# Filling products of a recurrence as four 64x64 quadrants over half the tokens, with three more tiles placed there

## The chip, the cores and the metric

The kernel runs on one core of one Trainium2 chip. The metric is the device time of the whole program in microseconds; the times shown are 3 runs of one and the same program. PE is TensorE, DVE is VectorE, ACT is ScalarE, POOL is GpSimd, SP is SyncE.

## The reference, cut to what matters

Two layers of a decoder trunk over 264 tokens (256 of a prompt and 8 samples). Per layer:

```
h = x @ w_in[l]                       # 2048 -> 10928 columns, all mixers' inputs and gates
rwkv_scan, per head and token:        # mixer A
    sa = S @ a_t
    S  = S * w_t + sa x b_t + v_t x k_t
    y  = S @ r_t
q, kc, vc, ks, vs, kw, vw, gl, z_b = split(fb)      # mixer B: attention, gated per head
merged = sigmoid(g_a) * (o_a @ w_up_a) + sigmoid(g_b) * (o_b @ w_up_b)
y = layer_norm(ALPHA * x + merged @ w_out)
```

Everything is float32. The change touches only how and when columns of `x @ w_in` are computed: those of the gate logits, the queries, z_b, some keys and values, and of g_b.

## The kernel before

A layer holds tokens along the free dimension (T = 264) and model columns on the 128 partitions. A tile is 128 output columns of `x @ w_in`: 16 products of 128x128 weights with 128x264 of XT, summed in one PSUM bank. I call one such product a k-step. A layer runs through these stages on PE:

1. two tiles (`two_tiles`), then 20 pairs of main tiles (`main_pair`);
2. the recurrence of mixer A, in chunks of 64 tokens, for four quads of two head pairs (`for hq in range(NQUAD)`). All its own products are 64x64 quadrants, except two groups at its start (64x128 and 128x128) and two with 32x32 blocks. Their steps are called low, bon, a1, tok, then y1 z1 to y5 z5 (a triangular inverse by doubling; y5 and z5 are the 32x32 ones), then for each of four chunks r, u, s, o;
3. the mixers' stage: the state update of the 8 samples on DVE (`rs`), a group norm, compression, attention of the prompt and of the samples (`as`);
4. gate pairs, up pairs and output pairs (`gate_pair` and so on), and the layer norm.

Steps of stages 2 and 3 depend on each other through ACT and DVE. So that PE isn't idle meanwhile, 44 more tiles of `x @ w_in` are filled in between: after each own step PE calls `project(L, ..., name)`, which goes on with the list TILES up to the k-step that the table UPTO names for that place. UPTO comes from the tables BEHIND (per quad), and BEHIND_MIX (mixers' stage). In the recurrence 20 tiles (EARLY) at most are used up, and the last call there, `project(L, "mixers")`, brings the count up to 20. The last call of the mixers' stage, `project(L, "gates")`, does what is left of the 46 tiles before the first gate pair.

A tile's bank is 6 or 7, by its number's parity, so the next tile can be summed while ACT empties the last one: `take_out` stands in ACT's program at the same named places, waits for `tile_done`, copies to H and raises `tile_out`. `mix` is DVE's counterpart, for the one tile that it mixes. The weights of a tile (1 MB) come through SP into one of two slots of WT, when the tile two before it is done.

Before the first gate pair stand, on the other engines: DVE's copy of the samples' outputs (L2227), two products that make z_b's output (L2230, L2233, the step `zb_v out`), SP's loads of the first pair's four weight blocks, which wait for that step since they overwrite the queries (L497), POOL's two sums of those blocks (L729 and L731, steps s3 and s1), and DVE's two (L2249, L2261, steps s2 and s4). The gate pair is seven products of 8 k-steps over 132 tokens: the first needs block 0, the second block 1, the third s3, the fourth s1, the fifth s2, the last s4.

Of the kernel before, what the change touches and what calls it, by code (L numbers as in the profile page):

```python
# [73 lines left out]
EARLY = 20  # L74
# [43 lines left out]
def plan():  # L118

    upto = {}  # L120
    for L in range(DEPTH):
        first = L * N_TILES * KT
        m = upto[L, "start"] = first + 2 * KT
        m = upto[L, "bc"] = m + 4
        for hq in range(NQUAD):
            for name, n in BEHIND.items():
                m = upto[L, hq, name] = min(m + n + (0 if name != "low" else 9 if hq == 0 else 2 * L), first + EARLY * KT)
        m = upto[L, "mixers"] = first + EARLY * KT
        for name, n in BEHIND_MIX.items():
            m = upto[L, name] = min(m + n, first + N_TILES * KT)  # L130
        upto[L, "gates"] = first + N_TILES * KT
    return upto

# [45 lines left out]
def hybrid_trunk(nc, ins, outs):  # L179
# [4 lines left out]
    with ExitStack() as ctx:  # L184
# [3 lines left out]
        def sem(name):  # L188
            return ctx.enter_context(nc.semaphore(name))
# [167 lines left out]
        scaled = sem("tile_scaled")  # L357
        S = {}
# [120 lines left out]
        def a_tile(L, kind, t):  # L479

            return VF[:, t - V0, :] if kind == "v" and L == 0 else H[:, t, :]

# [275 lines left out]
        def _(pe):  # L758
            mm, tr = nc.tensor.matmul, nc.tensor.transpose
            at = [0]  # L760
# [4 lines left out]
            def project(*place):  # L765

                while at[0] < UPTO[place]:
                    n, k = divmod(at[0], KT)
# [3 lines left out]
                    if k == 0:  # L772
# [3 lines left out]
                    if k == 8:  # L776
                        pe.wait_ge(w_in_slot[s][1], 16 * loads_of_slot(L, i, u))
                    rows, bank, start, stop = slice(0, P), 6 + s, k == 0, k == KT - 1
                    x = XT[:, k, :]
                    if kind == "gl":  # L780

                        rows, start, stop = slice(k % 2 * C, k % 2 * C + C), k < 2, k >= KT - 2
                    ins = mm(PB[rows, bank, 0:T], WT[:, s, k, 0:rows.stop - rows.start], x, start=start, stop=stop)  # L783
                    if k == KT - 1:
                        ins.then_inc(tile_done[s], 1)
                    at[0] += 1

            def two_tiles(L):
# [22 lines left out]
                at[0] += 2 * KT  # L811
# [181 lines left out]
            both = [slice(a * C, a * C + C) for a in range(2)]  # L993
# [11 lines left out]
            for L in range(DEPTH):  # L1005
# [161 lines left out]
                project(L, "mixers")  # L1167
# [265 lines left out]
        def _(sc):  # L1433
# [11 lines left out]
            def take_out(*place):  # L1445

                while (at[0] + 1) * KT <= UPTO[place]:
# [7 lines left out]
                    if kind == "lo":  # L1455
# [3 lines left out]
                    elif kind in ("kv", "q", "zb"):  # L1459
                        act(H[:, t, :], psum, ACT.Copy, scale=SCALE if kind == "q" else 1.0).then_inc(tile_out[s], 1)  # L1460
                    elif kind == "gl":
                        copy(H[:, t, :], psum).then_inc(tile_out[s], 1)
                    else:
                        if kind == "gb" and t == 9:
                            sc.wait_ge(*step("mix_t", L, "v3"))
                            sc.wait_ge(st_kv, 16 * (L + 1))
                        if kind == "ga" and t == 0:
                            sc.wait_ge(*step("gn_v", L, "out"))
                        act(H[:, t if kind == "ga" else GB_AT[t], :], psum, ACT.Tanh, scale=0.5).then_inc(tile_out[s], 1)  # L1469

            for L in range(DEPTH):
# [104 lines left out]
                take_out(L, "mixers")  # L1576
# [176 lines left out]
        def _(ve):  # L1753
            tt, ts, stt = nc.vector.tensor_tensor, nc.vector.tensor_scalar, nc.vector.scalar_tensor_tensor
            cp, red, recip = nc.vector.tensor_copy, nc.vector.tensor_reduce, nc.vector.reciprocal
            at, mixed = [0], [0]
# [4 lines left out]
            def mix(*place):  # L1761

                while (at[0] + 1) * KT <= UPTO[place]:
# [4 lines left out]
                    at[0] += 1  # L1768
                    if kind != "lo":
                        continue  # L1770
# [85 lines left out]
            for L in range(DEPTH):  # L1856
# [23 lines left out]
                for hq in range(NQUAD):  # L1880
# [41 lines left out]
                    v("rk", ins)  # L1922

# [18 lines left out]
                    mix(L, hq, "low")  # L1942
# [19 lines left out]
                    eight = lambda m: spread(small(m).unsqueeze(1), P, 2 * NCH, C)  # L1962
                    wait(("rw_t", "tok"))
# [5 lines left out]
                    for name in ("a1", "tok"):  # L1969
                        mix(L, hq, name)  # L1970
                    for j in range(1, LEVELS + 1):
# [15 lines left out]
                        else:  # L1987
# [4 lines left out]
                            v(f"z{j}", ins)  # L1992
                        mix(L, hq, f"z{j}")
                    if it:
                        ve.wait_ge(st_wkv, it * 32)
                    v("st", nc.vector.memset(ST[:, 0, :, :], 0.0))
# [13 lines left out]
                mix(L, "mixers")  # L2010
# [545 lines left out]
```

## Time and profile before

| | |
|---|---|
| runs | 2153.27, 2157.24, 2158.91 us (median 2157.24) |
| profiled execution | span 2153.9 us from the first to the last instruction; its whole time isn't reported apart |
| PE busy | 2119.7 us, 98% |
| DVE, POOL, ACT busy | 1060.1, 505.5, 412.9 us |
| granted TensorE clock | mean 0.995 |
| recurrence, both layers | about 281 to 510 us and 1346 to 1582 us |

How to read it: every float32 product has two records on PE, each with its weight load; both rows and counts below are of records, so a k-step of a filling tile is 2 records, and a 64x64 quadrant product 2 as well. Busy PE means that some record was under way; a record's duration contains its way through the array, and what a product costs in a row of products is the distance from start to start. For a merged row that is (its duration minus that of one record) divided by (count minus 1).

### The profile page before, as it was taken

How to read it: one execution, taken by the hardware profiler on the slowest of the kernel's cores; microseconds unless marked ns; L12 is line 12 of the kernel's file. 1: busy time of each engine (PE TensorE's matmuls, PEld its weight loads, DVE VectorE, ACT ScalarE, POOL GpSimd, SP SyncE). 2: the span in 40 equal slices, each digit the busy share in tenths (PEclk: the TensorE clock that was granted, in tenths of full speed). 3: DMA queues.
4: the chain of work that ended last, by engine and by line, in shares of the span. 5: the costliest groups of instructions: out<-in, count | busy, mean ns of one | idle time of the engine just before them, and what ended most of it. 6: DMA issues, size and time to landing. Idle time of an engine off the chain costs nothing.

```text
span 2153.9 us, 48812 instructions
## 1 busy us (share of the span) xinstructions
PE 2119.7 (98%) x21488; PEld 1870.9 (87%) x21488; DVE 1060.1 (49%) x1780; ACT 412.9 (19%) x1181; POOL 505.5 (23%) x377
## 2 busy tenths in 40 slices
PE   9999999999999999999999999999999999999997
PEld 8999977777887779999899999777777877899996
DVE  4454344443726524773645543444447165247745
ACT  1111112222103411110211121222221044111002
POOL 3433300002011123333223333000020112134331
PEclk9999999999999999999999999999999999999999
DMA  8545333335543365554355443332365334654551
GB/s 302 170 160 171 119 131 101 101 101 222 195 137 118 110 224 176 165 178 160 126 171 173 157 165 125 115 101 101 101 228 179 119 118 139 218 172 160 173 171 66
DMA packets 88979, 329.50 MB, mean 153 GB/s; under 512 B 11904, under 2 KB 11920, under 8 KB 86464
## 3 DMA queue, kind: packets, MB, share of 16 engines
q1 hardware_dynamic: 74592, 268.60, 37.2%
q0 software_dynamic: 11872, 53.59, 7.1%
q10 hardware_dynamic: 2304, 4.20, 0.6%
q8 instruction: 169, 2.77, 0.5%
q14 instruction: 42, 0.34, 0.1%
HBM read 315.91 MB, written 18.82 MB: 155 GB/s over the span
## 4 chain that ended last, share of the span: by engine, by line
PE 96%; DVE 3%; DMA 1%; issue 0%; ACT 0%; SPq 0%; DVEq 0%
PE PB L783 30%; PE PB L824 3%; PE PB L851 3%; PE PB L847 3%; PE PB L842 3%; PE PB L837 3%; PE PB L827 3%; PE PB L833 3%; PE PB L1239 3%; PE PB L763 1%; PE PB L907 1%; PE PB L989 1%; PE PB L808 1%; PE PB L972 1%; PE PB L974 1%; PE PB L967 1%
## 5 line engine op out<-in xcount | busy, mean ns | idle before, releaser
L783 PE MATMUL PB<-XT,WT 128*128 128x264 f32 (+1 forms) x2816 | 691.5, 395 | 0.1
L783 PEld LDWEIGHTS PB<-XT,WT 128*128 128x128 f32 (+1 forms) x2816 | 509.0, 189 | 101.0 <-issue 15.5
L1438 ACT ACTIVATE VT<-PB 128x132 f32<-128x132 f32 (+2 forms) x280 | 79.1, 291 | 578.3 <-PE PB L837 130.6
L1438 ACT ACTIVATE ARENA<-PB 128x128 f32<-128x128 f32 (+6 forms) x185 | 75.5, 430 | 226.0 <-PE PB L1089 62.2
L618 POOL DMA_DIRECT2D out<-in_c_win x16 | 8.1, 506 | 456.0 <-DVE ARENA L2005 456.0
L618 POOL DMA_DIRECT2D ARENA<-in_c_sel x64 | 40.0, 625 | 234.5 <-issue 234.5
L639 POOL TENSOR_TENSOR TOEP<-WT 128x1024 f32<-128x1024 f32 x20 | 47.3, 2365 | 181.0 <-PE PB L837 139.6
L639 POOL TENSOR_TENSOR TOEP<-H 128x1024 f32<-128x1024 f32 x20 | 48.2, 2408 | 139.5 <-PE PB L837 135.0
L833 PE MATMUL PB<-ARENA,TOEP 128*128 128x132 f32 x640 | 78.5, 276 | 0.0
L837 PE MATMUL PB<-ARENA,TOEP 128*128 128x132 f32 x640 | 78.5, 276 | 0.0
L842 PE MATMUL PB<-ARENA,TOEP 128*128 128x132 f32 x640 | 78.5, 276 | 0.0
L851 PE MATMUL PB<-XT,TOEP 128*128 128x132 f32 x640 | 78.5, 276 | 0.0
L833 PEld LDWEIGHTS PB<-ARENA,TOEP 128*128 128x128 f32 x640 | 75.1, 190 | 0.0
L837 PEld LDWEIGHTS PB<-ARENA,TOEP 128*128 128x128 f32 x640 | 75.1, 190 | 0.0
L842 PEld LDWEIGHTS PB<-ARENA,TOEP 128*128 128x128 f32 x640 | 75.1, 190 | 0.0
L851 PEld LDWEIGHTS PB<-XT,TOEP 128*128 128x128 f32 x640 | 75.1, 190 | 0.0
L1239 PE MATMUL PB<-ARENA 128*128 128x288 f32 x256 | 62.7, 406 | 0.0
L1842 DVE TENSOR_TENSOR VT<-PB,VT 128x264 f32<-128x264 f32 x40 | 17.3, 432 | 91.7 <-PE PB L851 91.7
L1239 PEld LDWEIGHTS PB<-ARENA 128*128 128x128 f32 x256 | 48.6, 190 | 13.3
L1644 ACT ACTIVATE ARENA<-ARENA 128x128 f32<-128x128 f32 (+1 forms) x128 | 56.2, 443 | 17.3 <-DVE ARENA L2164 17.3
L2336 DVE TENSOR_TENSOR VT<-VT 128x132 f32<-128x132 f32 x32 | 47.4, 1520 | 24.1 <-ACT VT L1438 24.1
L1469 ACT ACTIVATE H<-PB 128x264 f32<-128x264 f32 x48 | 18.7, 389 | 209.1 <-PE PB L783 208.9
(456 smaller groups left out, 4165.8 us busy)
## 6 DMA issues: line engine op xcount, KB each, us to landing
WT<-in_w_all SPq DMA_DIRECT2D x340, 512.0 KB, 4.5
H<-in_w_all SPq DMA_DIRECT2D x120, 512.0 KB, 4.5
KNVC<-in_w_all SPq DMA_DIRECT2D x40, 512.0 KB, 3.9
out<-in_c_win POOLq DMA_DIRECT2D x16, 512.0 KB, 4.6
ARENA<-in_c_cmp POOLq DMA_DIRECT2D x64, 128.0 KB, 4.3
ARENA<-in_c_sel POOLq DMA_DIRECT2D x64, 128.0 KB, 4.0
TOEP<-in_toep POOLq DMA_DIRECT2D x2, 2048.0 KB, 9.1
ARENA<-in_states POOLq DMA_DIRECT2D x4, 1024.0 KB, 11.9
```

What stands on the lines that cost most here:

```text
L639: mark("ms_p", it, add(OS1, w[2], w[3], ALU.add), "s1")
L783: ins = mm(PB[rows, bank, 0:T], WT[:, s, k, 0:rows.stop - rows.start], x, start=start, stop=stop)
L824: mm(a, w[0][:, k, :], XT[:, k, t0], start=k == 0, stop=k == BLK - 1)
L827: ins = mm(b, w[1][:, k, :], XT[:, BLK + k, t0], start=False, stop=k == BLK - 1, skip_group_check=True)
L833: mm(c, OS3[:, k, :], MT[:, 2, k, :], start=k == 0, stop=k == BLK - 1)
L837: ins = mm(d, OS1[:, k, :], MT[:, 0, k, :], start=False, stop=k == BLK - 1, skip_group_check=True)
L842: ins = mm(a, OS2[:, k, :], MT[:, 1, k, :], start=False, stop=k == BLK - 1, skip_group_check=True)
L847: ins = mm(c, w[3][:, k, :], MT[:, 3, k, :], start=False, stop=k == BLK - 1, skip_group_check=True)
L851: ins = mm(d, OS4[:, k, :], XT[:, BLK + k, t1], start=False, stop=k == BLK - 1, skip_group_check=True)
L1239: ins = mm(PB[:, 3 * (s // 8) + gp, 0:CMP_N], W1D[:, s, :], x, start=s % 8 == 0, stop=s % 8 == 7)
L1438: return act(out, in_, ACT.Copy)
L1644: ins = act(x, x, ACT.Exp, bias=NM[u % 3][:, t, i:i + 1], accum_out=RSM[u % 3][:, t, i:i + 1])
```

## The change

In tiles 3 to 22 of each layer (FIRST_QUAD to EARLY), `project` replaces a k-step by eight quadrant products: for each half of the tokens (132), each half of the 128 input rows and each half of the 128 output columns. The upper input rows sum into bank 6, the lower into bank 7. Progress is now counted in half k-steps (TILE = 32 of them). A tile now takes two operations out of PSUM: ACT copies bank 6 to H and raises `quad_half`, then DVE adds bank 7 to it and raises `tile_out`. Since a tile uses both banks, PE waits before each of these tiles, and before the one behind them, until the tile before is out. EARLY goes from 20 to 23, the tables of the recurrence are new, and so are the places where DVE's `mix` is called. The recurrence's own products are as before.

```
-EARLY = 20
+EARLY = 23
+FIRST_QUAD = 3
+TILE = 2 * KT
...
-BEHIND = {"low": 16, "bon": 4, "a1": 11, "tok": 7}
-for level in range(1, LEVELS + 1):
-    BEHIND.update({f"y{level}": 1 if level < LEVELS else 2, f"z{level}": 2 if level < LEVELS else 4})
+BEHIND = {"low": 32, "bon": 9, "a1": 23, "tok": 16}
+for level, (y, z) in enumerate(((3, 5), (3, 5), (0, 5), (3, 6), (5, 13)), 1):
+    BEHIND.update({f"y{level}": y, f"z{level}": z})
 for chunk in range(NCH):
-    BEHIND.update({f"r{chunk}": 1, f"u{chunk}": 1, f"s{chunk}": chunk // (NCH - 1)})
+    BEHIND.update({f"r{chunk}": 3 if chunk else 0, f"u{chunk}": 3, f"s{chunk}": chunk // (NCH - 1) * 11})
...
+                        if in_quadrants(n) or n and in_quadrants(n - 1):
+                            pe.wait_ge(tile_out[1 - s], (n - 1) // 2 + 1)
...
+                    if in_quadrants(n):
+                        tokens = slice(h * HALF, h * HALF + HALF)
+                        narrow = kind == "gl"
+                        for ra in both:
+                            for ca in both[k % 2:k % 2 + 1] if narrow else both:
+                                w = WT[ra, s, k, 0:C] if narrow else WT[ra, s, k, ca]
+                                ins = mm(PB[ca, 6 + ra.start // C, tokens], w, XT[ra, k, tokens], start=k <= narrow and h == 0,
+                                         stop=k >= KT - 1 - narrow and h == 1, skip_group_check=True)
...
# take_out, on ACT
+                    if in_quadrants(n):
+                        act(H[:, quad_home(kind, t), :], PB[:, 6, 0:T], ACT.Copy, scale=quad_scale(kind)).then_inc(quad_half, 1)
# mix, on DVE
+                    if in_quadrants(n):
+                        ve.wait_ge(quad_half, joined[0])
+                        stt(home, PB[:, 7, 0:T], quad_scale(kind), home, ALU.mult, ALU.add).then_inc(tile_out[s], 1)
...
# DVE, in a quad: mix(low) moves up, behind the products "rk", in quads 1 to 3
                     v("rk", ins)
+                    if hq:
+                        mix(L, hq, "low")
...
# the remainder of EARLY tiles behind the recurrence is gone
-                project(L, "mixers")
```

By the tables, the filling of quads 1 to 3 goes from 65 k-steps (67 in the second layer) to 160 half k-steps, which is 5 tiles, so that every one of these tiles ends at the end of a named place: low, a1, z2, z5 and s3. In quad 0 tile 2, still whole, ends within the place low.

The first place, on PE: the end of the doubling and the chunks of quad 1 in the first layer (L1144 and L1172 are the steps r, L1150 and L1178 the steps u, L783 and L806 the filling). Before:

```order
L783 MATMUL PB<-XT,WT 128x264 x4
L1144 MATMUL PB<-ARENA 64x64 x4
L783 MATMUL PB<-XT,WT 128x264
L1150 MATMUL PB<-ARENA 64x64 x4
L783 MATMUL PB<-XT,WT 128x264
L1156 MATMUL PB<-ARENA 64x64 x4
L1160 MATMUL PB<-ARENA 64x64 x4
L1163 MATMUL PB<-ARENA 64x64 x4
```

And now:

```order
L806 MATMUL PB<-XT,WT 64x132 x52
L1172 MATMUL PB<-ARENA 64x64 x4
L1178 MATMUL PB<-ARENA 64x64 x4
L806 MATMUL PB<-XT,WT 64x132 x12
L1184 MATMUL PB<-ARENA 64x64 x4
L1188 MATMUL PB<-ARENA 64x64 x4
L1191 MATMUL PB<-ARENA 64x64 x4
```

What moved: 4 whole k-steps before r0 are 13 halves (52 quadrant products), the filling between r0 and u0 is gone, and that behind u0 is three halves in place of a k-step.

The second place, on DVE: the start of quad 1 (L1921 and L1956 are the products "rk", which step bon waits for; L1934 and L1971 the last one that step a1 waits for). Before:

```order
L1921 SCALAR_TENSOR_TENSOR ARENA<-H,PT,ARENA 128x264 x2
L1927 SCALAR_TENSOR_TENSOR ARENA<-KNVC,ARENA 128x4x64 x2
L1931 TENSOR_TENSOR ARENA<-H,ARENA 128x4x64 x2
L1933 TENSOR_TENSOR ARENA<-ARENA 128x512
L1934 TENSOR_TENSOR ARENA<-ARENA 128x512
```

And now:

```order
L1956 SCALAR_TENSOR_TENSOR ARENA<-H,PT,ARENA 128x264 x2
L1803 SCALAR_TENSOR_TENSOR H<-PB,H 128x264
L1964 SCALAR_TENSOR_TENSOR ARENA<-KNVC,ARENA 128x4x64 x2
L1968 TENSOR_TENSOR ARENA<-H,ARENA 128x4x64 x2
L1970 TENSOR_TENSOR ARENA<-ARENA 128x512
L1971 TENSOR_TENSOR ARENA<-ARENA 128x512
```

What moved: the addition that empties bank 7 (L1803) stands among the operations that step a1 waits for.

The third place, on PE: the end of the samples' attention and the first gate pair (L763 there is the transposition whose result DVE copies back, L865 the first product of the pair). Before:

```order
L1382 MATMUL PB<-KNVC,ARENA 32x256 x4
L783 MATMUL PB<-XT,WT 128x264 x3
L763 MATMUL PB<-CM,ARENA 128x128 x2
L783 MATMUL PB<-XT,WT 128x264 x49
L865 MATMUL PB<-XT,H 128x132 x8
L868 MATMUL PB<-XT,H 128x132 x8
```

And now:

```order
L1409 MATMUL PB<-KNVC,ARENA 32x256 x4
L813 MATMUL PB<-XT,WT 128x264 x3
L781 MATMUL PB<-CM,ARENA 128x128 x2
L813 MATMUL PB<-XT,WT 128x264
L894 MATMUL PB<-XT,H 128x132 x8
L897 MATMUL PB<-XT,H 128x132 x8
```

What moved: of the 49 k-steps ahead of the gate pairs 48 are gone into the recurrence. The places between are as they were.

## Rows read from the trace of the kernel before

**Rows 1.** The page: busy times, and the chain that ended last by engine.

```profile
PE 2119.7 (98%) x21488; PEld 1870.9 (87%) x21488; DVE 1060.1 (49%) x1780; ACT 412.9 (19%) x1181; POOL 505.5 (23%) x377
PE 96%; DVE 3%; DMA 1%; issue 0%; ACT 0%; SPq 0%; DVEq 0%
```

**Rows 2.** Timeline of PE, chunks of the recurrence: start, us, engine, line, operands, count.

```profile
385.56 0.45 PE L1150 MATMUL PB<-ARENA 64*64 64x64 f32 x8
385.94 0.71 PE L783 MATMUL PB<-XT,WT 128*128 128x264 f32 x2
386.58 0.45 PE L1156 MATMUL PB<-ARENA 64*64 64x64 f32 x8
386.86 0.40 PE L1160 MATMUL PB<-ARENA 64*64 64x64 f32 x8
```

**Rows 3.** Timeline of PE: quadrants of 128 columns, and 98 whole records.

```profile
295.70 1.98 PE L1070 MATMUL PB<-ARENA 64*64 64x128 f32 x64
...
785.07 21.97 PE L783 MATMUL PB<-XT,WT 128*128 128x264 f32 x98
806.88 1.96 PE L865 MATMUL PB<-XT,H 128*128 128x132 f32 x16
```

**Rows 4.** Timeline of PE and ACT: the filling behind y3, and ACT's copy of y3.

```profile
373.48 0.71 PE L783 MATMUL PB<-XT,WT 128*128 128x264 f32 x2
...
373.61 0.38 ACT L1438 ACTIVATE VT<-PB 128x256 f32<-128x256 f32 x1 [3.50 <-PE PB L1102]
```

**Rows 5.** Timeline of DVE and PE: the start of quad 1, first layer.

```profile
347.56 0.90 DVE L1921 SCALAR_TENSOR_TENSOR ARENA<-H,PT,ARENA 128x264 f32<-128x264 f32 x2
...
350.32 0.69 DVE L1934 TENSOR_TENSOR ARENA<-ARENA 128x512 f32<-128x512 f32 x1
...
351.65 1.98 PE L1070 MATMUL PB<-ARENA 64*64 64x128 f32 x64
```

**Rows 6.** Timeline of PE and DVE: the filling of low in a quad, second layer.

```profile
1526.96 8.17 PE L783 MATMUL PB<-XT,WT 128*128 128x264 f32 x36
...
1533.96 0.90 DVE L1921 SCALAR_TENSOR_TENSOR ARENA<-H,PT,ARENA 128x264 f32<-128x264 f32 x2
```

**Rows 7.** Timeline of PE and ACT: the filling of low in quad 0, both layers.

```profile
281.71 11.39 PE L783 MATMUL PB<-XT,WT 128*128 128x264 f32 x50
...
289.28 0.37 ACT L1460 ACTIVATE H<-PB 128x264 f32<-128x264 f32 x1
...
1348.77 11.29 PE L783 MATMUL PB<-XT,WT 128*128 128x264 f32 x50
...
1357.48 0.37 ACT L1460 ACTIVATE H<-PB 128x264 f32<-128x264 f32 x1
```

**Rows 8.** Timeline of PE and DVE: from the recurrence to the samples' state update.

```profile
509.55 7.39 PE L783 MATMUL PB<-XT,WT 128*128 128x264 f32 x32
...
571.14 0.19 DVE L2046 COPY ARENA<-ARENA 64x64 f32<-64x64 f32 x1
...
571.66 0.27 PE L763 MATMUL PB<-CM,ARENA 64*128 64x64 f32 x1
...
1582.07 4.72 PE L783 MATMUL PB<-XT,WT 128*128 128x264 f32 x20
```

**Rows 9.** Timeline of DVE, SP and POOL ahead of the first gate pair.

```profile
788.56 2.36 DVE L2233 SCALAR_TENSOR_TENSOR H<-H,ARENA 128x2112 f32<-128x2112 f32 x1
...
793.68 0.43 SPq L497 DMA_DIRECT2D H<-in_w_all  x1
...
801.34 2.35 POOL L729 TENSOR_TENSOR TOEP<-H,KNVC 128x1024 f32<-128x1024 f32 x1 [30.86 <-DMA KNVC<-in_w_all]
803.80 2.35 POOL L731 TENSOR_TENSOR TOEP<-KNVC 128x1024 f32<-128x1024 f32 x1
```

**Rows 10.** L497's loads; then a stretch: engines' busy times, granted clock, DMA share.

```profile
DMA to landing us min/median/max: 3.1/4.3/9.6
...
661.00:670.00 9.00, 9.00 (x83) 7.58 (x83) 4.26 (x16) 0.65 (x3) 6.67 (x10) 0.81 0.91 286
```

More of the change, by code:

```diff
@@ L121, in plan, with in_quadrants @@
     for L in range(DEPTH):
-        first = L * N_TILES * KT
-        m = upto[L, "start"] = first + 2 * KT
-        m = upto[L, "bc"] = m + 4
+        first = L * N_TILES * TILE
+        m = upto[L, "start"] = first + 2 * TILE
+        m = upto[L, "bc"] = m + TILE - HEAD_LOW
         for hq in range(NQUAD):
             for name, n in BEHIND.items():
-                m = upto[L, hq, name] = min(m + n + (0 if name != "low" else 9 if hq == 0 else 2 * L), first + EARLY * KT)
-        m = upto[L, "mixers"] = first + EARLY * KT
+                m = upto[L, hq, name] = m + n + (HEAD_LOW if name == "low" and hq == 0 else 0)
+        assert m == first + EARLY * TILE
         for name, n in BEHIND_MIX.items():
-            m = upto[L, name] = min(m + n, first + N_TILES * KT)
-        upto[L, "gates"] = first + N_TILES * KT
-    return upto
+            m = upto[L, name] = min(m + 2 * n, first + N_TILES * TILE)
+        upto[L, "gates"] = first + N_TILES * TILE
+    return upto
+def in_quadrants(n):
+    return FIRST_QUAD <= n % N_TILES < EARLY
 UPTO = plan()
@@ L481, in a_tile, with quad_home, quad_scale @@
             return VF[:, t - V0, :] if kind == "v" and L == 0 else H[:, t, :]
+        def quad_home(kind, t):
+            return GB_AT[t] if kind == "gb" else t
+        def quad_scale(kind):
+            return {"q": SCALE, "gb": 0.5}.get(kind, 1.0)
         block = ctx.enter_context(nc.Block())
@@ L759, in _ @@
             mm, tr = nc.tensor.matmul, nc.tensor.transpose
+            both = [slice(a * C, a * C + C) for a in range(2)]
             at = [0]
@@ L771, in project @@
                     s, u = n % 2, n // 2
-                    if k == 0:
+                    at[0] += 1
+                    if k == 0 and h == 0:
                         pe.wait_ge(w_in_slot[s][0], 16 * loads_of_slot(L, i, u))
@@ L1445, in take_out @@
             def take_out(*place):
-                while (at[0] + 1) * KT <= UPTO[place]:
+                while (at[0] + 1) * TILE <= UPTO[place]:
                     n = at[0]
@@ L1454, in take_out @@
                     psum = PB[:, 6 + s, 0:T]
-                    if kind == "lo":
+                    if in_quadrants(n):
+                        act(H[:, quad_home(kind, t), :], PB[:, 6, 0:T], ACT.Copy, scale=quad_scale(kind)).then_inc(quad_half, 1)
+                        if kind == "gb":
+                            sc.wait_ge(tile_out[s], u + 1)
+                            gate = H[:, GB_AT[t], :]
+                            act(gate, gate, ACT.Tanh)
+                    elif kind == "lo":
                         if kind == "lo" and L == 0:
@@ L1761, in mix @@
             def mix(*place):
-                while (at[0] + 1) * KT <= UPTO[place]:
+                while (at[0] + 1) * TILE <= UPTO[place]:
                     n = at[0]
@@ L1941, in _ @@
                         wait("vm")
-                    mix(L, hq, "low")
+                    if hq == 0:
+                        mix(L, hq, "low")
                     wait(("rw_t", "bon"))
@@ L1968, in _ @@
                     v("lm1", tt(LM[:, :, :], LT[:, :, :], eight(LV0 + 1), ALU.mult))
-                    for name in ("a1", "tok"):
-                        mix(L, hq, name)
+                    mix(L, hq, "tok")
                     for j in range(1, LEVELS + 1):
```

36 lines of the change are left out of this document (18 added, 18 removed).

## The prediction

> **What bounds the kernel now.** I read the page first: PE is busy for 98% of the span and makes 96% of the chain that ended last, DVE 49% [rows 1]. So what counts is time on PE: work there, and every wait that becomes PE's. Then the timeline of PE in the recurrence, where the distances between starts tell what "busy" hides.
>
> A filling record (half a k-step, 264 columns) in a long row costs (21.97 - 0.39) / 97 = 0.2225 us, so a k-step 0.445 [rows 3]. In a visit of a single k-step between 64x64 products it takes 385.94 to 386.58 = 0.64 us, 0.195 more. And the eight own records ahead of it take 385.56 to 385.94 = 0.38 us, where eight ahead of another group of 64x64 products take 386.58 to 386.86 = 0.28 [rows 2]. A change between whole products and quadrants and back thus costs 0.195 + 0.10 = 0.295 us. The waits between a step and the next are hidden by the filling in between, so the change can only gain from these switches and from the speed of the products; everything else that is moved must give back the same time elsewhere, or less.
>
> **The change part by part.**
>
> 1. The switches. Per quad, 21 groups of 64x64 or 32x32 products stand between whole filling now: a1, tok, five y, five z, and nine in the chunks. The 19 that aren't 32x32 lose their switch. Step bon is 128x128 and today needs none; it gains one. So 18 x 0.295 = 5.3 us per quad, over 8 quads -42.5 us. No row shows a change between 64x64 and 32x32, which y5 and z5 now meet: its price lies between 0 and a whole one, and I take the whole (0.295 less for each would be -4.7 in all). A group's gain I bound by 0.23 (if 0.06 stays at each border of quadrants) and 0.33.
> The Trainium skill, TensorEngine Tiling (Array Packing), section Key Properties, says that changing the tiling mode, not just the tile, drains the engine. That is the 0.295 of the rows above, and it makes the change to 32x32 a change of mode too; by that rule the sum stands, without it the sum would be 4.7 us lower.
>
> 2. The speed of the quadrants. The trace has them with 128 columns: (1.98 - 0.27) / 63 = 0.0271 us from start to start, weights loaded anew each time, four quadrants in turn [rows 3]. With 132 columns 0.0280; half a k-step is 4 products, 8 records, 0.2236 us, where a whole record costs 0.2225. 1280 halves x 0.0011 = +1.4. Bounds: 0.220, and 8 x 1.91 / 64 x 132 / 128 = 0.246 if I divide all the time of that group by its count (-3 to +30); the start-to-start value is the nearer one, since the rest of the group's time is its switch.
>
> 3. Places left empty. Behind y3 and r0 no filling stands any more. ACT's copy of y3 starts 0.13 us after the filling behind it and ends at 373.99. With quadrants the next product could start 0.10 before 373.48, at about 373.38 [rows 4], so PE waits 0.65 with the way of the signal. At r0 ACT first empties bank 6 (0.37), then copies; about the same. 2 x 0.65 x 8 = +10.4; bounds 0.5 and 0.9 each.
> At the other places three halves (0.67) stand for a visit of 0.64, five for two k-steps: the time is as before, with more filling in it. The nine halves behind bon and the 16 behind tok likewise.
>
> 4. Emptying tiles. A tile out of its two banks is ACT's copy, 0.37, then DVE's addition, which I take at 0.45 (the two of rk, the same form on 264 columns, take 0.90 together [rows 5]), 1.2 us with signals. PE waits for it only where a tile has ended, and there its own step comes first: low, tok and y3 take over 1 us each. Covered, but for two places:
>  (a) quads 1 to 3: the addition stands between rk and the operations that a1 waits for. First layer: rk is ready at 348.46, the last of them at 351.01, a1 starts at 351.65 [rows 5]. The 32 halves end about 348.95, ACT's copy 349.6, the addition 350.05; the remaining operations take 351.01 - 348.46 = 2.55 and end at 352.6, while PE, with bon and its switch (0.98) and nine halves (2.1), is there at 352.05: it waits 0.6. Second layer: 36 records become 32 halves, which end at 1534.2, and rk is ready only at 1534.86 [rows 6]: 0.7. 6 x 0.65 = +3.9 (0 to 6.6).
>  (b) quad 0: tile 2, still whole, ends inside place low, and tile 3 may start only when it is out, but ACT takes it out at the end of its own part. First layer: 24 records end at 281.71 + 5.34 + 0.1 = 287.15, ACT's copy at 289.65. Second: 1354.2 against 1357.85 [rows 7]. With the signal 2.55 + 3.7 = +6.2. Queued behind that wait are 32 halves and then bon, for which everything waits, so it counts whole.
>
> 5. Less filling behind the recurrence. The 32 records (first layer) and 20 (second) between the last own product and the mixers' stage were 7.22 and 4.55 us, now 11 halves and a switch, 2.55. PE comes 4.7 and 2.0 us earlier to the product that waits for DVE's state update. That update hangs on loads that start from the end of the recurrence, so it is not earlier. Today it ends at 571.33, PE's product starts at 571.66, 0.25 of it slack [rows 8]. So PE waits 4.5 + 1.8 = +6.3, if the second layer has the same slack.
>
> 6. The 48 k-steps ahead of the gate pairs. They were cover too. The transposition ends where the 98 records start, 785.07; z_b's output is ready at 788.56 + 2.36 = 790.92, 5.85 later; only then may SP load the first pair's blocks. Today SP comes to it at 793.68, behind the last tile's weights, POOL starts s3 7.66 later, and s1 ends at 806.15, just before PE is there at 806.88 [rows 9]. Now SP issues at 5.9 after the transposition. For the first two blocks I take 5.8 us, between the median landing of 4.3 [rows 10] and 7.66. s3 starts at 11.7, s1 ends 4.81 later at 16.5, and the fourth product, which needs s1, starts at 16.55. Four products of 1.80 (16 records of (1.96 - 0.28) / 15 = 0.112 us) follow [rows 3]: the pair ends at 23.8. Without a wait it would start at 0.55 and end at 13.15. So PE loses 10.6 us. Its first product stands still until about 10.3, and after idling like that the clock may be low: in a stretch behind thin work it was granted 0.81 over 9 us [rows 10], that is 3.4 us at 1.2 in place of 2.4 GHz. Half of 3.4 is 1.7, of which 0.85 goes into the wait for s1. I take 11.5 per layer, 23.0 in all; with 4.3 for the blocks 9.1, with 7.66 and a low clock 13.5.
>
> The sum: -42.5 + 1.4 + 10.4 + 3.9 + 6.2 + 6.3 + 23.0 = +8.7 us. The filling itself, 44 tiles per layer, is the same on both sides. Against the profiled execution it makes a span of 2153.9 + 8.7 = 2162.6; that span is 3.3 below the median of the runs (2157.2), and against the median it is 2165.9. **Forecast: 2166 us.**
>
> **The rivals.**
>
> A. Faster: the switches weigh more and the new waits less. The point is the waits at the gate pairs and at the state update: if the weight blocks land in 4.3 us (2 x 2.4 less), the switch to 32x32 is free (-4.7) and a group gains 0.33 (-5.0), with the waits for ACT at 0.5 (-2.4), the sum is 8.7 - 16.9 = -8, 2149. For it: PE is the bound, and 42 us of switches are real in the rows. Against: five things must go one way. Its pivot is the gate pairs: it holds once items 3 to 6 cost under 34 us together, in place of 49.8.
>
> B. No change: half of that, the gate pairs at 9.5 each and little at a1: -5 to -10 from the forecast, 2158.
>
> C. Much slower: the quadrants of the filling come at 0.246 per half (item 2, the whole group's time divided): +30 less what waits they fill, some 5: 2191. Against: the records inside the group.
>
> D. The change does not do what it says: filling and own products in quadrants still don't overlap because the filling sums in the same banks again and again, so 0.1 stays at each border of 38 per quad: +30 too, 2195. For it: groups that follow each other on quadrants today start 0.05 behind the last record, not 0.03. Against: that 0.05 is already in my 0.28.
>
> **How the numbers follow.** The forecast has 0.52, A 0.16, B 0.24, C and D together 0.08. The forecast's own range, from the bounds of single terms, is 2159 to 2175; for 8 times in 10 I take A's and B's times in, and a part of C: 2148 to 2182. No change means within 0.3%, 6.5 us, about what runs of this kernel can tell apart. Faster than 2150.8: A's better part and some of the unexpected, 0.17. Between 2150.8 and 2163.7: B, and the forecast's lower edge, 0.26. Slower: 0.57.
>
> **What would show it.** In the profile after: 16 records of a 64x132 filling product in 0.445 us, and eight own records ahead of them in 0.28 to 0.30 instead of 0.38 (1, 2). PE idle behind y3 and r0 for ACT, some 0.6 each (3). The first two rows of filling in quad 0 with 2.5 and 3.7 us idle between them (4b). The product at the end of the state update with 4 and 2 us of idle before it, released by DVE (5). Between the transposition and the gate pair's first product 10 us with one k-step in them, released by the weights' DMA, a second wait for POOL, and a low clock behind it (6). I am wrong if the gate pair starts at once, for then its blocks were loaded earlier than their table of waits lets me believe, or if a quad of the first layer grows by much more or less than 15 x 0.445 - 5.3 + 0.2 + 1.3 + 0.6 = 3.5 us.

## The result and the profile after

The changed kernel takes 2282.0 us in the median of 4 runs (2273.2 to 2284.5) beside 2157.3 for the kernel before: ratio 1.0566, interval 1.0542 to 1.0590. I had forecast slower, but 8.7 us slower; it is 125. The profiled execution has a span of 2271.3 us, 117.4 above that of before. Medians, ranges and ratios below leave out two runs in which the chip ran slow: one of e5 (2487.8 us, mean granted clock 0.956) and one of the kernel before, taken beside e1 to e4 (3623.8 us, 0.555).

The page of the changed kernel, to be read against [rows 1]: the lines of the busy times, of the queue that brings instructions, of the chain that ended last, and of the filling in quadrants.

```profile
span 2271.3 us, 66262 instructions
PE 2130.5 (94%) x30192; PEld 1955.5 (86%) x30192; DVE 1079.6 (48%) x1820; ACT 414.0 (18%) x1183; POOL 505.3 (22%) x377
q8 instruction: 237, 3.88, 0.7%
PE 84%; DVE 8%; issue 4%; DMA 2%; ACT 1%; POOL 0%; SPq 0%; DVEq 0%; ACTq 0%; POOLq 0%
L806 PE MATMUL PB<-XT,WT 64*64 64x132 f32 x9984 | 354.5, 284 | 41.0 <-issue 34.6
```

Two things are new. The chain has 4% "issue", where PE waited for nothing that the profile shows; before it had 0%. And the filling line alone has 34.6 us of such idle time. The page of before has 48812 instructions and 169 packets on the instruction queue:

```profile
q8 instruction: 169, 2.77, 0.5%
```

What PE waited for, by line, in the changed kernel (us in total, times, longest), the eleven largest:

```profile
PE PB L806 <- issue: 34.6, 27, 3.7
PE PB L894 <- DMA H<-in_w_all: 18.6, 2, 9.5
PE PB L1141 <- issue: 7.7, 6, 2.6
PE PB L1130 <- issue: 6.3, 5, 2.4
PE PB L806 <- ACT H L1493: 6.2, 2, 3.7
PE PB L1158 <- issue: 6.1, 7, 1.3
PE PB L1098 <- issue: 4.7, 2, 2.6
PE PB L1155 <- ACT VT L1465: 4.0, 9, 0.5
PE PB L781 <- DVE ARENA L2083: 3.7, 2, 2.1
PE PB L781 <- DVE ARENA L2223: 3.6, 2, 1.8
PE PB L1178 <- ACT ARENA L1465: 3.3, 8, 0.4
```

Five of the rows are the waits that the prediction named (ACT at tile 3, ACT behind y3 and r0, DVE's state, the weights at the gate pair), and the one for L2223 is in the kernel before too, with the same 3.6. The five "issue" rows were named by nobody, and they stand in filling and in own products alike: in the middle of a row of records on the same banks and tiles. Here is one, in the timeline of PE, the filling of low in quad 1 of the first layer:

```profile
356.33 5.62 PE L806 MATMUL PB<-XT,WT 64*64 64x132 f32 x188
363.76 2.24 PE L806 MATMUL PB<-XT,WT 64*64 64x132 f32 x68 [1.81 <-issue]
```

188 records run at their pace ((5.62 - 0.27) / 187 = 0.0286 us; without a disturbance it is 0.0279), then nothing for 1.81 us, then the rest. **These stalls stand at one place of PE's instruction stream.** Stretches whose edges lie in the middle of four such stalls (two pairs of neighbours), in a row of busy times with the counts of records and weight loads:

```profile
387.00:391.00 4.00, 2.64 (x128) 2.50 (x128) 0.69 (x1) 0.00 (x0) 0.00 (x0) 1.00 0.02 4
391.00:395.00 4.00, 2.97 (x128) 2.68 (x128) 1.38 (x2) 0.38 (x1) 0.00 (x0) 1.00 0.02 4
403.00:407.20 4.20, 3.15 (x128) 2.86 (x128) 0.69 (x1) 0.00 (x0) 0.00 (x0) 1.00 0.02 4
407.20:411.20 4.00, 3.58 (x128) 3.08 (x128) 0.97 (x3) 0.38 (x1) 0.00 (x0) 1.00 0.01 4
```

From stall to stall there are 128 records and 128 weight loads, 256 instructions, in 4 us, whatever steps they belong to. I counted PE's records, weight loads and waits for semaphores over the whole trace: of 49 distances over 0.5 us between two records of one line, 43 stand at two neighbouring places of the count modulo 256 (192 and 193), through both layers. A packet of the instruction queue has 16 KB, so 256 instructions are 64 bytes each; from the kernel before to the changed one the page's count of instructions grew by 17450 and that of the packets by 68, one for 257. In 56 such stalls over 0.5 us the last packet had landed 1.38 us (median) before PE went on, and the next packet set off 1.15 us (median) after. With 0.9 to 1.4 for the packet itself that is a round of 3.4 to 3.9 us; in quads 0 to 2 of the first layer the packets are 3.73 us apart in the median and never under 3.33. 128 pairs of filling records want a new block every 3.57 us (128 x 0.0279), steps like tok or y, with a record per 0.015 us, every 1.9 us. PE runs out of instructions.

The Trainium skill, Runtime: NRT & Kernel Launch, section Instruction fetch mechanics, says that an engine's instructions come in blocks of 16 KiB, 256 instructions, over a queue that the sequencer drives; the trace agrees, with packets of 16 KB and stalls 256 instructions apart. The same section of the Trainium skill says that crossing such a boundary is "mostly hidden", because instructions are issued more slowly than they are filled in; here the measurement differs and decides: at 14 ns an instruction and faster it isn't hidden, and the stalls come to 88 us (the table below).

**The rest of the loss in the recurrences is the clock.** The stall of 3.0 us at 433.36 and the stretch behind it (columns: PE, PEld, DVE, ACT and POOL busy, granted clock, DMA share, GB/s):

```profile
433.30:436.40 3.10, 0.37 (x14) 0.15 (x7) 2.77 (x6) 1.73 (x7) 0.00 (x0) 1.00 0.29 114
436.40:440.00 3.60, 3.60 (x71) 3.60 (x74) 0.00 (x0) 0.00 (x0) 0.00 (x0) 0.53 0.02 5
```

After standing still PE is granted 0.53, the lower of its two levels but for a remainder, and 71 records take 3.6 us in place of 2.0. In the two recurrences 47.8 us pass at the low level; in the kernel before none. Of the 47.8, 41.0 stand behind stalls at a block's edge and 6.8 behind the two waits for ACT at tile 3 (from 289.75 and from 1423.0). The clock doesn't fall each time: of the 12 stalls over 2 us, it stayed up behind three (at 363.8, 523.8 and 1587.7).

This stall is one of 12 over 2 us, and its cause has a second half: the next tile's weights. SP issued their two loads at 428.39. The DMA engines' busy share in the 15 us from 425 to 440, in 40 slices (tenths):

```profile
DMA  0100009900099009999799883120000001000000
```

The weights' transfer (from slice 15, counted from 0, which is 430.6, to about 434.5) fills the engines. The instruction packet that PE needs sets off only at 433.9, 8.4 us behind the one before it. PE had begun on the last block it had at 429.68; the packet set off 4.3 us behind that, where 1.15 is the median. The stall ends at 436.36.

### The profile page after: what moved, and what is told of

It is laid out like the page before. It is cut to its first block, busy times and chain, and to the rows that moved or that the text cites. A ratio compares the mean times of both kernels' runs of the same rounds, so it can differ in the third digit from the quotient of the medians.

```text
span 2271.3 us, 66262 instructions
## 1 busy us (share of the span) xinstructions
PE 2130.5 (94%) x30192; PEld 1955.5 (86%) x30192; DVE 1079.6 (48%) x1820; ACT 414.0 (18%) x1183; POOL 505.3 (22%) x377
## 4 chain that ended last, share of the span: by engine, by line
PE 84%; DVE 8%; issue 4%; DMA 2%; ACT 1%; POOL 0%; SPq 0%; DVEq 0%; ACTq 0%; POOLq 0%
PE PB L806 13%; PE PB L813 10%; PE PB L853 3%; PE PB L880 3%; PE PB L876 3%; PE PB L862 3%; PE PB L871 3%; PE PB L866 3%; PE PB L856 3%; PE PB L1266 3%; PE PB L936 1%; PE PB L1018 1%; PE PB L1001 1%; PE PB L1003 1%; PE PB L965 1%
## 5 line engine op out<-in xcount | busy, mean ns | idle before, releaser
L806 PE MATMUL PB<-XT,WT 64*64 64x132 f32 x9984 | 354.5, 284 | 41.0 <-issue 34.6
L813 PE MATMUL PB<-XT,WT 128*128 128x264 f32 x1536 | 363.1, 390 | 1.5 <-DMA WT<-in_w_all 1.5
L806 PEld LDWEIGHTS PB<-XT,WT 64*64 64x64 f32 x9984 | 308.6, 139 | 55.4 <-issue 54.2
L813 PEld LDWEIGHTS PB<-XT,WT 128*128 128x128 f32 x1536 | 285.8, 191 | 59.0 <-issue 11.8
L2012 DVE TENSOR_TENSOR ARENA<-ARENA,CM 128x512 f32<-128x512 f32 x32 | 22.2, 693 | 85.3 <-PE PB L1130 50.5
```

Of the source, the lines that this page charges most:

```text
L806: ins = mm(PB[ca, 6 + ra.start // C, tokens], w, XT[ra, k, tokens], start=k <= narrow and h == 0, stop=k >= KT - 1 - narrow and h == 1, sk ...
L813: ins = mm(PB[:, 6 + s, 0:T], WT[:, s, k, :], XT[:, k, :], start=k == 0, stop=k == KT - 1)
```

## The experiments

The table counts the two recurrences together, each from its first product of low to the first transposition behind it. "At the block's edge" is the sum of the distances over 0.1 us between records at number 191 to 193 of 256. The clock's column is half of the time at the low level, an upper bound of what it costs, so "rest" is a lower bound; in the kernels with quadrants everywhere it takes in the low clock behind the waits at tile 3 as well (3.4 us of cost at most in the changed kernel and in e4). Each ratio is taken against runs of the kernel before made beside that experiment: their medians are 2157.4 us for e1 to e4, 2160.5 for e5 to e7 and 2157.8 for e8 and e9.

| kernel | time (us, median) | PE instructions per filling k-step there | recurrences | at the block's edge | clock | rest |
|---|---|---|---|---|---|---|
| before | 2157 | 4 | 476.5 | 6.4 | 0 | 470.1 |
| e2, whole products, changed placement | 2202.9 | 4 | 529.0 | 13.5 | 0 | 515.5 |
| e1, quadrants of 264 | 2215.6 | 16 | 547.9 | 38.3 | 15.3 | 494.3 |
| e3, mixed | 2229.3 | 24 | 556.9 | 52.6 | 8.5 | 495.8 |
| e4, 1/8 of the bytes | 2228.1 | 32 | 566.4 | 67.6 | 5.1 | 493.7 |
| changed | 2282.0 | 32 | 602.5 | 88.0 | 23.9 | 490.6 |

**e1: quadrants over all tokens.** In the branch of the quadrants:

```diff
-                        tokens = slice(h * HALF, h * HALF + HALF)
                         narrow = kind == "gl"
+                        if h:
+                            continue
...
-                                ins = mm(PB[ca, 6 + ra.start // C, tokens], w, XT[ra, k, tokens], start=k <= narrow and h == 0,
-                                         stop=k >= KT - 1 - narrow and h == 1, skip_group_check=True)
+                                ins = mm(PB[ca, 6 + ra.start // C, 0:T], w, XT[ra, k, 0:T], start=k <= narrow,
+                                         stop=k >= KT - 1 - narrow, skip_group_check=True)
```

> Fetch theory: PE runs out of instructions. In the changed kernel PE's stalls in the quadrants stand 256 records apart, and blocks of 16 KB come no faster than one per 3.75 us, while 128 pairs of weight load and product at 27.9 ns take 3.57. With 264 tokens per quadrant product a k-step has 16 records of PE and its weight loads' lane in place of 32 for the same time in the array, so a block lasts 7.1 us of filling. The stalls without a semaphore nearly go; of the 125 us too much, some 85 of gaps and 15 of low clock behind them go too: 2165 to 2190. Rivals: quadrant products are slow by themselves (banks, weight loads), or the drains by ACT and DVE hold PE: then it stays at 2260 to 2290. The moved filling is to blame (gate pairs without cover): 2250 to 2290 as well.

Measured: 2215.6 us (2212.5 to 2221.1), ratio 1.0267, interval 1.0248 to 1.0285. Half of the instructions of the filling gone takes away 66 us: the fetch theory's direction and against the rivals, but 25 us short of its range. What is left are 21 stalls over 0.5 us at the edge, about half of them in steps y and z: 128 instructions in each step and 32 in the two k-steps behind each make 320 in 3.8 us, still faster than the fetch (3.73 for 256 would be 4.66 for 320). I had looked at the filling's pace only; own products were too fast all along, and the whole filling products between them were what let the fetch catch up.

**e2: the placement alone.** FIRST_QUAD becomes N_TILES, so every tile is whole; the gate logits' tile gets its whole form back.

```diff
-FIRST_QUAD = 3
+FIRST_QUAD = N_TILES
...
-                    ins = mm(PB[:, 6 + s, 0:T], WT[:, s, k, :], XT[:, k, :], start=k == 0, stop=k == KT - 1)
+                    rows, start, stop = slice(0, P), k == 0, k == KT - 1
+                    if kind == "gl":
+                        rows, start, stop = slice(k % 2 * C, k % 2 * C + C), k < 2, k >= KT - 2
+                    ins = mm(PB[rows, 6 + s, 0:T], WT[:, s, k, 0:rows.stop - rows.start], XT[:, k, :], start=start, stop=stop)
...
```

> The changed placement (three more tiles ahead, the new table, the addition's place in DVE) with whole 128x128 filling products everywhere, 264 tokens, taken out by ACT alone. The switches come back (+42.5 by my sum), the quadrants' 1.4, the addition behind rk (3.9) and the wait at tile 2 (6.2, in part) go. Fetch theory: 2157 + 8.7 + 42.5 - 1.4 - 3.9 = 2204, range 2185 to 2215, with stalls as few as in the kernel before. If the placement were what costs the 125 us, it would be 2280 or more.

Measured: 2202.9 us (2199.6 to 2205.7), ratio 1.0211, interval 1.0192 to 1.0229. A hit for the time. The placement alone costs 45 us, as the sum had it, and is not the cause of the other 80. Only the stalls aren't as few as in the kernel before: 13.5 us at the edges for 6.4. The waits at the gate pairs and at the state update are all here (waits of PE in this kernel):

```profile
PE PB L897 <- DMA H<-in_w_all: 19.3, 2, 9.6
PE PB L781 <- DVE ARENA L2088: 7.8, 2, 4.8
```

**e3: half of the k-steps wide.**

```diff
-                        tokens = slice(h * HALF, h * HALF + HALF)
+                        if k % 2 and h == 0:
+                            continue
+                        tokens = slice(0, T) if k % 2 else slice(h * HALF, h * HALF + HALF)
...
```

> Quadrants, but in every odd k-step over all 264 tokens and in every even one over half, in two goes: 24 records and weight loads per k-step of 0.445 us on average, so 256 instructions last 4.75 us of filling in place of 3.57. Fetch theory: filling alone no longer outruns the fetch, own products still do: a third of the excess is left, 2195 to 2225. If it is the quadrants as such: 2260 to 2290, as before. Linear in the number of instructions would be the middle between this kernel's and the wide one's time.

Measured: 2229.3 us (2228.3 to 2235.6), ratio 1.0343, interval 1.0321 to 1.0365: 4 us above the range, far below the rival, and well under the middle of the two (2249). So it isn't linear in the number of instructions, as a price per instruction or per product would be; what costs is the part of the stream that outruns the fetch.

**e4: the same instructions, fewer bytes beside them.** Of tiles 5 to 24 one eighth of the weights is loaded:

```diff
                 for half in range(2):
-                    sp.dma_start(WT[:, s, 8 * half:8 * half + 8, :], w_all[L, i, :, 8 * half:8 * half + 8, :]).then_inc(w_in_slot[s][half], 16)
+                    n_k = 1 if 5 <= i < 25 else 8
+                    sp.dma_start(WT[:, s, 8 * half:8 * half + n_k, :], w_all[L, i, :, 8 * half:8 * half + n_k, :]).then_inc(w_in_slot[s][half], 16)
```

> The changed kernel, but of the weights of tiles 5 to 24 of each layer only the first of eight blocks per half is loaded (1/8 of the bytes; the rest of the slot keeps what was there, so the values are others). If the instruction blocks are late because they share the DMA engines with the weights, the stalls over 2 us go and the time falls to 2200 to 2240. If the fetch has a fixed latency of about 3.7 us per block in an idle DMA too, only the long ones shrink: 2255 to 2275. If the cause is in PE or in the drains: unchanged, 2275 to 2285.

Measured: 2228.1 us (2226.0 to 2231.4), ratio 1.0330, interval 1.0312 to 1.0348, so 54 us less than the changed kernel, within the range of "late because they share the DMA engines". The waits of PE on the filling there:

```profile
PE PB L807 <- issue: 17.3, 23, 1.5
```

Nearly as many stalls in the filling as without the edit (23 for 27), but the longest is 1.5 us in place of 3.7: none over 2 us at an edge is left, and the low clock in the recurrences went from 47.8 to 10.2 us, of which 6.8 stand behind the two waits at tile 3. Yet 67.6 us at the edges stay. So both expectations were half right: the fetch has a round of its own (packets 3.81 us apart in the median in nearly idle DMA engines), and weights in front of it make it longer. Between the two profiled executions the gain is 44.5 us: 36.1 in the recurrences, 8.4 outside them, where the wait for DVE's state (3.7) is gone; for the other 4.7 I know no cause.

**e5: more instructions without quadrants.** In the kernel before, filling of the recurrence in quarters:

```diff
-                    ins = mm(PB[rows, bank, 0:T], WT[:, s, k, 0:rows.stop - rows.start], x, start=start, stop=stop)
+                    for a in range(4 if 2 <= i < EARLY else 1):
+                        part = slice(a * 66, a * 66 + 66) if 2 <= i < EARLY else slice(0, T)
+                        ins = mm(PB[rows, bank, part], WT[:, s, k, 0:rows.stop - rows.start], x[:, part], start=start and a == 0,
+                                 stop=stop and part.stop == T, skip_group_check=True)
```

> The kernel before, with no quadrants and its own placement, but each whole filling product of the recurrence in four products of 66 tokens: same columns for the array, 16 records and weight loads per k-step in place of 4. Fetch theory: in the long rows nothing changes (256 instructions last 7 us there). In a level of the inversion a step y and a step z with three k-steps hold 256 + 12 = 268 instructions in 3.88 us now; with 304 they need 304/256 x 3.75 = 4.45 us: 0.57 x 4 levels x 8 quads = 18 us, less where the buffer has a reserve: 2163 to 2178, with stalls one block of 256 instructions apart in the steps y and z. If the fetch doesn't matter without quadrants: 2154 to 2161. If a whole record of 66 columns is bound by its weight load, the long rows slow down too, which the distance between records there shows.

Measured: 2398.6 us (2393.4 to 2424.0), ratio 1.1117, interval 1.1081 to 1.1153. A miss, and of little use for the question: a record of 66 columns over the full array takes as long as one of 132. I put that down to the weight load that each record has; no run shows it apart. Its timeline:

```profile
395.83 10.04 PE L785 MATMUL PB<-XT,WT 128*128 128x66 f32 x88
```

(10.04 - 0.3) / 87 = 0.112 us from start to start, the same as for 132 columns [rows 3]. At that pace the fetch is seldom late (34 packets in the first three quads, 6.4 us apart in the median, with two stalls over 0.5 us at an edge, 1.84 at 338.8 in a step y and 0.76 at 345.7 in a step z). Whether instructions outrun the fetch in a kernel whose filling has no quadrants is thus not shown by an experiment; this trace and that of the kernel before show it at a few places only.

**e6: fewer bytes in the kernel before.** The edit of e4 there.

> The kernel before, but of the weights of tiles 5 to 24 of each layer only the first of eight blocks per half is loaded (1/8 of the bytes, the values are others). The control to the same edit in the changed kernel, which gave 54 us there. Fetch theory: the kernel before has hardly a stall, so there is nothing to win: 2150 to 2159. If the weights' transfers hold PE in another way than by the instruction blocks, it gains here as well: under 2140.

Measured: 2153.2 us (2152.0 to 2156.5), ratio 0.9976, interval 0.9964 to 0.9988: by the ratio 5 us, as expected, where the same edit gave 54 in the changed kernel. So the weights' transfers hold PE in the recurrence by way of the instructions.

**e7: quadrants only where the fetch has room.** On the kernel before: k-steps behind r, u and s are quadrants over 264 tokens, all others whole and into the tile's own bank; the second bank takes only the lower half of those quadrants, and DVE adds it. A tile with quadrants waits for the other bank at its first quadrant, and the next tile until DVE has added. The table is shifted by single k-steps, so that such a tile ends in the chunks; in quads 1 to 3 no filling stands behind the last chunk any more.

```diff
+        for (L, *place), end in UPTO.items():
+            if len(place) == 2 and place[1][0] in QUAD_ROWS and place[1] not in ("y5", "z5"):
+                found.update(range(last, end))
...
+                    if at[0] in QUAD_STEPS:
+                        first = not any(m in QUAD_STEPS for m in range(n * KT, at[0]))
+                        if first:
+                            pe.wait_ge(tile_out[1 - s], (n - 1) // 2 + 1)
+                        for ra in both:
+                            bank = 6 + (s if ra.start == 0 else 1 - s)
+                            for ca in both:
+                                ins = mm(PB[ca, bank, 0:T], WT[ra, s, k, ca], XT[ra, k, :], start=k == 0 or (first and ra.start > 0),
...
```

> The kernel before with quadrants of 264 tokens only in the rows of filling in the chunks (behind r, u and s: 66 k-steps in all, in 4 tiles of a layer, which ACT and DVE join), all other filling whole, 20 tiles ahead of the mixers as before; the table is shifted by single k-steps so that such a tile ends with the last chunk. A step of the chunks has 8 records, so PE takes far fewer instructions there than the fetch brings: no stall. Two visits per chunk lose their switch, of which ACT's copies (0.66 from own records to the next step) leave 0.2 each: 2 x 4 x 8 x 0.2 = -13 us; joining costs up to 0.5 at each of 8 tiles: 2144 to 2152. If quadrants cost something by themselves (banks, the join) it is not below 2157. With the whole 0.295: 2140.

Measured: 2151.3 us (2148.4 to 2158.0), ratio 0.9965, interval 0.9951 to 0.9979: faster than the changed kernel by far, and than the kernel before by 0.35%, a small gain but clear of the noise. Its timeline, one chunk from r to the next r and the start of the next quad:

```profile
396.56 0.38 PE L1177 MATMUL PB<-ARENA 64*64 64x64 f32 x5
...
397.38 0.38 PE L1183 MATMUL PB<-ARENA 64*64 64x64 f32 x5
...
398.21 0.45 PE L1189 MATMUL PB<-ARENA 64*64 64x64 f32 x8
398.49 0.40 PE L1193 MATMUL PB<-ARENA 64*64 64x64 f32 x8
398.72 0.40 PE L1196 MATMUL PB<-ARENA 64*64 64x64 f32 x8
400.13 0.46 PE L1085 MATMUL PB<-ARENA,WA 64*128 64x264 f32 x1 [1.01 <-DVE ARENA L2044]
```

From r to u and from u to s it is 0.82 us each; before, u to s took 385.56 to 386.58 = 1.02 [rows 2]. That is the 0.2 expected for each of the 64 visits (the median over them is 0.825 for 1.021), so 12.5 us were won. About a third is given back in the last row: with no filling behind the last chunk, PE waits for DVE's last state, four times about 1 us. The recurrences have 472.2 us, 4.3 less than before: the stalls at the edges grew by 2.9 and the low clock costs up to 1.7.

**e8: one and a half k-steps in the rows of r and u.** Half of a k-step over 132 tokens behind r, its other half behind u; four k-steps of each quad moved there:

```diff
-    BEHIND.update({f"r{chunk}": 1, f"u{chunk}": 1,
+    BEHIND.update({f"r{chunk}": 2, f"u{chunk}": 1,
...
+                        half = len(place) == 3 and place[2][0] == "r" and at[0] == UPTO[place] - 1
+                        if half:
+                            carried.append((n, k))
+                        ins = quadrants(n, k, slice(0, HALF if half else T), first)
```

> The kernel with quadrants in the chunks only, but one and a half k-steps behind each r and each u in place of one (one over all tokens and one half: 32 records and weight loads instead of 16), and one k-step behind the last chunk. Four k-steps per quad come from the rows of bon, a1, tok and z5, where DVE and ACT had slack. In the chunk's rows PE waits about 0.2 us for ACT's copy with one k-step; half a k-step (0.22) fills it, so 4 k-steps per quad go at next to no cost: -4 x 0.445 x 8 = -14, and the row behind the last chunk -3: 2133 to 2141. A chunk has 80 + 64 instructions in 2.7 us, 19 ns each, under the fetch's pace of 3.75/256 = 14.6: no stalls. If the rows that gave k-steps were tight, or the fetch already counts here, 2145 to 2155.

Measured: 2150.0 us (2142.7 to 2156.2), ratio 0.9960, interval 0.9943 to 0.9976. Its median is the lowest of all, though its interval overlaps that of e7. The recurrences have 464.3 us, 8 less than in e7, where 17 were expected. The half k-steps weren't free: from r to u it is 0.954 us and from u to s 0.903 in the median, for 0.825 in e7, which is 6.6 us over the 32 chunks. About 5 more are at the blocks' edges (14.2 in place of 9.3): five stalls of 1.2 to 2.6 us, all in steps y and z. The two make somewhat more than the 9 that are missing. "No stalls" was wrong: the chunks themselves have none, but the steps y and z, which had just enough, get their instructions later. That the chunks' larger use is what makes them late is my reading; no run shows it apart.

**e9: a k-step behind the last chunk.** One k-step from z5 to s3, on e7.

> The kernel with quadrants in the chunks only, with one k-step moved from z5 (whole) to behind the last chunk (quadrants), where PE stood for 0.9 us longer than before it in each quad for ACT's copy. 0.445 + 0.1 of those 0.9 are filled: -0.5 x 8 = -4 against that kernel: 2145 to 2149. Nothing else changes.

Measured: 2153.5 us (2148.6 to 2159.5), ratio 0.9981, interval 0.9969 to 0.9993. A miss: no gain over e7 (recurrences 472.8 against 472.2). The wait that I blamed on ACT was DVE's, and it is gone. But in the last quad of each layer whole filling now follows the joined tile at once and waits 1.1 us for DVE's addition (2.2 in all), and quad 0 of the second layer grew by 3 us, which I didn't settle.

## Why the prediction was wrong

The steps, by the prediction's numbers. In the last column of the table the recurrences without stalls and clock have 490.6 us. The forecast made the recurrences 476.5 + 42.7 (three tiles of 16 k-steps, twice) - 42.5 + 1.4 + 10.4 + 3.9 + 6.2 = 498.6, with the 6.4 of stalls that before has: 492.2 without. So steps 1 to 4 together were right to 2 us in the changed kernel, if the low clock costs its upper bound; errors of single steps may cancel in that. A quad of the first layer was to grow by 3.5 us; quads 1 and 2 grew by 16.4 and 22.1.

1. **The switches: right in kind, their size shown only roughly.** In an undisturbed place the groups follow each other without a gap. Whole products against quadrants of 264, by the rest column: 515.5 - 494.3 = 21 us, where 42.5 less what quadrants cost elsewhere (1.4, 3.9, 6.2) makes 31; 8 of the 10 between them come from e2, whose rest is 8 under my sum for it. Of those, 4.7 are a slip in that sum: behind y3 and r0 no filling stands in e2 either, so 2 of the 18 switches don't come back there (2 x 0.295 x 8). The others I can't place. Steps y5 and z5 kept their switch at both ends, as taken.
2. **The speed of the quadrants: the step that failed.** The pace of 0.0279 us per record was right (0.0280 forecast), and the bound of 0.246 per half (rival C) wrong. But I priced 1280 halves by the array alone. Each brings 16 instructions where a whole k-step brings 4, and the bounds of -3 to +30 had no term for bringing them. The runs show in its place 81.6 us more of stalls at the blocks' edges (88.0 - 6.4) and up to 20.5 for the clock that falls behind them: 102.1 of the 103.9 by which the recurrences exceed the forecast.
3. **Empty places: right.** Behind y3 PE stands from start to start for 0.69 us, behind r0 for 0.64, in nearly each quad: 10.6 for 10.4.
4. **Emptying tiles.** DVE's addition takes 0.43 (0.45 forecast). (a) was mis-sized: a1 and bon wait 1.6 us in all for DVE, not 3.9, since PE came late itself. (b) was right: 6.2 in the row of waits, for 6.2. I left out the clock behind it, up to 3.4 us in both layers:

```profile
289.58 9.10 PE L806 MATMUL PB<-XT,WT 64*64 64x132 f32 x256 [2.48 <-ACT H L1493]
```

256 records at 0.0279 are 7.1 and took 9.0.

5. **The state update: mis-sized,** 3.7 us instead of 6.3; in e2, with few stalls, 7.8.
6. **The gate pairs: right in mechanism, a little small.** The first product of the pair stands for 9.47 us in the first layer:

```profile
867.46 3.89 PE L894 MATMUL PB<-XT,H 128*128 128x132 f32 x16 [9.47 <-DMA H<-in_w_all]
```

The next pair starts at 883.56 and, in the second layer, at 2008.77. Without a wait a pair takes 12.6 from the end of the filling (857.98, 1983.69): 13.0 and 12.5 us lost, 25.5 for 23.0. The low clock costs more than I took: the first two products of the pair take 6.60 us (867.46 to 874.06) for 3.60. The second wait, for POOL's s1, didn't come; a short one for DVE's s2 did (0.3 and 0.9). Outside the recurrences the changed kernel gains 4.2 us per layer, where the tiles that moved out are 21.4; so 17.2 are lost per layer, 34.4 in both. Steps 5 and 6 are 29.2 of them; 5 I can't place.

The rivals: neither C nor D came; a cause that no rival named made the size. Yet the page of before had what was needed: 21488 records and as many weight loads of PE [rows 1], and on the instruction queue 2.77 MB in 169 packets. Dividing would have given 16 KB and 254 instructions; the chunk and level steps of the timeline would have given the pace at which PE eats them. In before, a level of the inversion takes 3.9 us (two own steps of 128 instructions, and 12 for three k-steps): 268 instructions at 14.5 ns, just what the fetch brings (3.73 / 256 = 14.6). By that count there was nothing to win from the filling in that level, and instructions added there had to cost time.

## What to carry to other kernels

Count instructions as a resource of their own: where PE's timeline, as here, packs more than 256 of them into some 3.7 us for longer than a block or two, the instruction queue is the bound, not the array, and a finer tiling of the same work makes it worse. Long instructions between short ones are then more than filling: they are where the fetch catches up, so small tiles pay only where the engine waits for others anyway (here behind r and u, 0.2 us each). "issue" time in the middle of a group that repeats every 256 instructions is the sign to look for.

## What the runs showed of the hardware

- Instructions of PE come in packets of 16 KB; back to back they are 3.3 to 3.8 us apart, so about 13 to 15 ns per instruction, and PE goes on 1.38 us after one has landed.
- These packets wait for weights on the same DMA engines: stalls of up to 3.7 us with the weights' loads beside them, up to 1.6 with an eighth of their bytes (e4).
- Most long stalls cost more than their length, by the clock granted behind them: 0.53 in the 3.6 us behind one of 3.0 us. In the recurrences of the changed kernel 41.0 us at the low level stand behind stalls at an edge, 3.4 with short stalls (e4), none in the kernel before.
- A record over the full array with new weights took 0.112 us, whether it had 66 or 132 columns; on 64x64 quadrants, four in turn, 0.0279 for 132 columns and 0.015 for 64 or fewer.
- Own products of 32x32 between quadrants of 64x64 pay for the switch as they do between whole products: with 264 columns in the filling, 0.31 us from the start of its last record to y5 in e1 (quadrants) and 0.32 in the kernel before (whole). In the changed kernel, with 132 columns, it is 0.20, where own products of 64x64 follow a filling record at 0.05 in the median.
